# Final LayerNorm of a decoder layer in two parts: all tokens first, the last expert block's rows as a ninth tile, with the second pass of three tiles on TensorE

## What is computed

```python
def layer_norm(x, g, b):
    mu = jnp.mean(x, axis=-1, keepdims=True)
    xc = x - mu
    var = jnp.mean(xc * xc, axis=-1, keepdims=True)
    return xc * lax.rsqrt(var + LN_EPS) * g + b

m = grouped_moe(x, w_router, b_router, w_up, w_down)   # top-2 experts of each token, weighted sum
x = layer_norm(DEEPNORM_ALPHA * x + m, ln2_g, ln2_b)
```

## Time and profile before

| what | value |
|---|---|
| median of 3 runs | 1670.3 us (1667.24 to 1670.33) |
| profiled execution, its own time | 1669.88 us |
| its span (first to last instruction) | 1668.2 us |
| PE busy | 1596.2 us (96%) |
| DVE busy | 1176.0 us (70%) |
| ACT busy | 845.4 us (51%) |
| mean granted TensorE clock | 0.977 of full speed |
| last matmuls of the last block, start | 1623.15 us |
| last second pass on DVE, start | 1663.78 us |

### The profile page before, as it was taken

One profiled execution on the slowest core, in us unless ns is written; L12 is line 12 of the kernel. 1 busy time (PEld: TensorE's weight loads), 2 busy tenths in 40 slices (PEclk: granted clock), 3 DMA queues, 4 the chain that ended last, 5 costly groups with the idle time before them and its releaser, 6 DMA issues.

```text
span 1668.2 us, 20247 instructions
## 1 busy us (share of the span) xinstructions
PE 1596.2 (96%) x7711; PEld 1321.9 (79%) x7711; DVE 1176.0 (70%) x1472; ACT 845.4 (51%) x1174; POOL 183.5 (11%) x219
## 2 busy tenths in 40 slices
PE   7999999999999999999999997999999999999981
PEld 6788888888888888888788885788888888888770
DVE  3755868495666666332575666799999999998884
ACT  3113121214556555325221333688888888887773
POOL 0000000202212220000000001111111111111120
PEclk9999999999999999999999997999999999999995
DMA  5144534645232331411553566899999999999966
GB/s 160 39 82 73 128 71 85 79 73 158 80 112 66 108 87 59 145 46 49 169 176 123 174 221 235 338 369 377 370 359 357 353 353 357 351 344 365 350 237 215
DMA packets 156985, 329.29 MB, mean 197 GB/s; under 512 B 15919, under 2 KB 85551, under 8 KB 156890
## 3 DMA queue, kind: packets, MB, share of 16 engines
q1 hardware_dynamic: 140746, 289.69, 53.8%
q0 software_dynamic: 16144, 38.32, 7.7%
HBM read 296.74 MB, written 48.52 MB: 207 GB/s over the span
## 4 chain that ended last, share of the span: by engine, by line
PE 88%; DMA 6%; DVE 3%; issue 1%; SPq 1%; ACT 1%; POOLq 0%; DVEq 0%; ACTq 0%
PE ps L753 53%; PE ps L1050 26%; DMA e_raw<-in_w_down 3%; PE ps L854 2%; PE ps L839 2%; PE ps L1057 1%; DMA e_raw<-in_w_up 1%; DVE e_lo L1868 1%; PE ps L998 1%; PE ps L1063 1%; DMA x_raw<-in_x 1%; DVE zout L1928 1%; DVE zout L1921 1%; PE ps L986 0%; SPq L547 0%
## 5 line engine op out<-in xcount | busy, mean ns | idle before, releaser
L1868 DVE TENSOR_TENSOR e_lo<-e_raw,e_hi 128x1024 fp32r<-128x1024 f32 x376 | 436.2, 1221 | 24.4 <-ACT e_hi L1364 20.8
L1364 ACT ACTIVATE e_hi<-e_raw 128x1024 fp32r<-128x1024 f32 x376 | 367.8, 1050 | 25.3 <-DMA e_raw<-in_w_down 17.9
L753 PE MATMUL ps<-xt_hi,w_hi 128*128 128x512 f32 x896 | 303.3, 395 | 2.4 <-DVE xt_lo L1467 2.4
L753 PE MATMUL ps<-xt_lo,w_hi 128*128 128x512 f32 x896 | 299.0, 390 | 0.0
L753 PE MATMUL ps<-xt_hi,w_lo 128*128 128x512 f32 x896 | 298.8, 390 | 0.0
L753 PEld LDWEIGHTS ps<-xt_hi,w_lo 128*128 128x128 f32 x896 | 168.4, 188 | 35.9
L753 PEld LDWEIGHTS ps<-xt_hi,w_hi 128*128 128x128 f32 x896 | 168.3, 189 | 35.2 <-DVE xt_lo L1467 2.6
L753 PEld LDWEIGHTS ps<-xt_lo,w_hi 128*128 128x128 f32 x896 | 168.8, 188 | 33.0
L1500 DVE TENSOR_TENSOR w_lo<-w_raw,w_hi 128x512 fp32r<-128x512 f32 x136 | 94.9, 703 | 130.8 <-ACT w_hi L1133 127.4
L1133 ACT ACTIVATE w_hi<-w_raw 128x512 fp32r<-128x512 f32 x136 | 83.7, 628 | 202.1 <-PE ps L753 199.6
L1050 PE MATMUL ps<-e_hi,xe_hi 128*128 128x512 f32 x512 | 164.4, 402 | 8.5 <-DVE e_lo L1868 7.9
(11 more groups left out here) (280 smaller groups left out, 2254.7 us busy)
## 6 DMA issues: line engine op xcount, KB each, us to landing
e_raw<-in_w_up SPq DMA_DIRECT2D x128, 1024.0 KB, 21.9
e_raw<-in_w_down SPq DMA_DIRECT2D x64, 1024.0 KB, 21.7
w_raw<-in_w_in SPq DMA_DIRECT2D x64, 256.0 KB, 4.9
w_raw<-in_w_gate SPq DMA_DIRECT2D x48, 256.0 KB, 3.5
gates_d<-gate_t POOLq DMA_DIRECT2D x16, 512.0 KB, 3.4
gate_s<-gates_d SPq DMA_DIRECT2D x16, 512.0 KB, 3.6
qkv_d<-qkv POOLq DMA_DIRECT2D x12, 512.0 KB, 3.8
w_raw<-in_w_branch SPq DMA_DIRECT2D x24, 256.0 KB, 3.7
```

The costliest lines, as they stand in the source:

```text
L753: last = nc.tensor.matmul(o(h, c1 - c0), st(k), mv(k, c0, c1), start=start and k == nk[0] and n == 0, stop=h in stop and k == nk[-1] and n ...
L1364: nc.scalar.activation(e_hi[:, (UPT + s) % RSPL, :], e_raw[r][:, s % 2, :], ACT.Copy).then_inc(e_h, 1)
L1868: nc.vector.tensor_tensor(e_lo[:, sp_, :], e_raw[raw_slot(b, s)][:, s % 2, :], e_hi[:, sp_, :], ALU.subtract).then_inc(e_all, 1)
```

## The change

The final LayerNorm's start no longer waits for the last block's scatter, which is gone: the loads of the eight tiles wait for the scatters up to the block before the last one. ACT writes the last block's result to a buffer of its own, `ye_last`. POOL gathers the last block's token rows of `z_d` into `zlate`, DVE adds `ye_last`, and these rows go through the LayerNorm as a ninth tile. Its result is written by an indirect transfer over those rows of `out`, after the eight plain stores have landed. For tiles 0, 2 and 4 the second pass moves from DVE to PE: ACT makes a 128x128 matrix with the reciprocals on its diagonal (`diagonal`), PE writes b (as ones times the row b) plus that matrix times the first pass's result to PSUM, in halves of 512 columns, and ACT copies the result to `zout` (`take_z`). The stores have the order 1, 3, 0, 5, 2, 6, 7, 4. ACT's load of the square-root table moves ahead of the last `result`. Buffers move to make room (`zin`, `zout`, `zsq`, `zst`), and two semaphores are merged into others (`xg_zero`, `std9`).

```diff
+ADD_AT = 5
+ON_PE = (0, 2, 4)
+STORES = (1, 3, 0, 5, 2, 6, 7, 4)
...
-            sp.wait_ge(ye_out, 16 * (last_b + 1))
+            sp.wait_ge(e_all, item(STATIC, 0))
+            sp.wait_ge(ye_out, 16 * last_b)
             for t in range(TT):
                 sp.dma_start(zin[:, t, :], z_d[t * P:(t + 1) * P, :]).then_inc(tile_in[t], 16)
-            for t in range(TT):
-                sp.wait_ge(out_ok, t + 1)
-                sp.dma_start(out[0, t * P:(t + 1) * P, :], zout[:, t, :]).then_inc(out_dma[t % 4], 16)
+            for i, t in enumerate(STORES):
+                if t in ON_PE:
+                    sp.wait_ge(evac[0], 1 + CT * len(KINDS) // 2 + ON_PE.index(t) + 1)
+                else:
+                    sp.wait_ge(out_ok, t + 1 - sum(u < t for u in ON_PE))
+                sp.dma_start(out[0, t * P:(t + 1) * P, :], zout[t][:]).then_inc(out_dma[i % 4], 16)
...
-            for k in range(3):
+            for k in range(2):
                 scatter(tail + 1 + k)
+            pool.wait_ge(row_ok, tail + 2)
+            pool.sem_inc(passed, 1)
+            nc.gpsimd.tensor_copy(row_l[:], tok_tab[:, bass.ds(tail + 2, 1)]).then_inc(row_ok, 1)
...
+            pool.wait_ge(ye_out, 16 * (tail + 2))
+            pool.sem_inc(passed, 1)
+            nc.gpsimd.indirect_dma_start(out=zlate[:], out_offset=None, in_=z_d,
...
+            for u in range(4):
+                pool.wait_ge(out_dma[u], 16 * TT // 4)
+            pool.wait_ge(out_ok, TT + 1 - len(ON_PE))
+            nc.gpsimd.indirect_dma_start(out=out[0], out_offset=bass.IndirectOffsetOnAxis(ap=row_l[:], axis=0),
+                                         in_=zout[TT][:], in_offset=None,
...
+            for i, t in enumerate(ON_PE):
+                pe.wait_ge(z_diag, i + 1)
+                if i >= 2:
+                    pe.wait_ge(evac[0], 1 + CT * len(KINDS) // 2 + i - 1)
...
+                for h in range(2):
+                    o = ps[:, z_bank(t) + h, :]
+                    nc.tensor.matmul(o, ones_e[0:1, 0:1].to_broadcast([1, P]), lnb2[0:1, h * HALF:(h + 1) * HALF], start=True, stop=False)
+                    last = nc.tensor.matmul(o, z_rstd[i][:], zout[t][:, h * HALF:(h + 1) * HALF], start=False, stop=True)
+                last.then_inc(z_mm, 1)
...
-            result(tail + 3, UPT, 0)
-
             nc.scalar.activation(zst[:, 0, 5:6], eps[:], ACT.Sqrt)
...
+            result(tail + 3, UPT, 0, ye_last)
...
+            def diagonal(t):
+                act.wait_ge(ln9, recips(t))
+                nc.scalar.activation(z_rstd[ON_PE.index(t)][:], ident[:], ACT.Copy, scale=zst[:, t, 4:5]).then_inc(z_diag, 1)
+
+            def take_z(t):
+                act.wait_ge(z_mm, ON_PE.index(t) + 1)
+                nc.scalar.activation(zout[t][:], flat(z_bank(t)), ACT.Copy).then_inc(evac[0], 1)
+
+            deviation(0)
+            deviation(1)
+            diagonal(0)
+            deviation(2)
+            deviation(3)
+            diagonal(2)
+            deviation(4)
+            deviation(5)
+            take_z(0)
+            deviation(6)
+            diagonal(4)
+            deviation(7)
+            take_z(2)
+            deviation(TT)
+            take_z(4)
...
+            def second_pass(t):
+                dve.wait_ge(std6, TT + t + 1)
+                done.go(nc.vector.reciprocal(zst[:, t, 4:5], zst[:, t, 3:4]))
+                if t in ON_PE:
+                    assert done.n == recips(t)
+                    return
+                done.join()
+                nc.vector.scalar_tensor_tensor(zout[t][:], zout[t][:], zst[:, t, 4:5], lnb2[:], ALU.mult, ALU.add).then_inc(out_ok, 1)
...
+            for t in range(1, TT):
+                if t == ADD_AT:
+                    dve.wait_ge(late_in, 16)
...
+                    done.go(nc.vector.tensor_tensor(zlate[:], zlate[:], ye_last[:], ALU.add))
...
+                first_pass(t)
+                second_pass(t - 1)
+            second_pass(TT - 1)
+            first_pass(TT)
+            second_pass(TT)
```

More of the change, by code:

```diff
@@ L76 @@
 O_PIECE = 8
+ADD_AT = 5
+ON_PE = (0, 2, 4)
+STORES = (1, 3, 0, 5, 2, 6, 7, 4)
+LN9_ADDED = 2 * ADD_AT
 ALPHA = 2.0 ** 0.25
@@ L245, in program @@
         tok_i = at("tok_i", [P, 1], I32, 203.875)
+        row_l = at("row_l", [P, 1], I32, 205.90625)
         row_i = at("row_i", [P, 1], I32, 203.90625)
@@ L261, in program @@
         x1_scaled = at("x1_scaled", [P, D], FP32, 76)
[L262 to L265, removed]
+        zin = at("zin", [P, TT, D + 1], FP32, 79.75)
+        zlate = at("zlate", [P, D + 1], FP32, 160)
+        z_rstd = [at(f"z_rstd{i}", [P, P], FP32, 144 + i / 2) for i in range(len(ON_PE))]
+        ye_last = at("ye_last", [P, D + 1], FP32, 169)
+        zout = [at(f"zout{i}", [P, D], FP32, kb) for i, kb in enumerate((184, 188, 192, 196, 132, 136, 64, 68, 176))]
+        zsq = at("zsq", [P, D], FP32, 140)
+        zst = at("zst", [P, TT + 1, 16], FP32, 202)
         lng2 = at("lng2", [P, D], FP32, 124)
@@ L319, in program @@
         out_ok, out_dma = sem("out_ok"), [sem(f"out_dma{u}") for u in range(4)]
-        std3, std6, std9 = sem("std3"), sem("std6"), sem("std9")
+        std3, std6 = sem("std3"), sem("std6")
+        z_diag, z_mm = sem("z_diag"), sem("z_mm")
         passed = sem("passed")
@@ L351, in program, with recips, z_bank, z_tile @@
             assert raw_count(STATIC, _s) == STATIC - RTURN
+        def recips(t):
+            return 3 + 2 * t + (t + 1 >= ADD_AT)
+        def z_bank(t):
+            return 4 + 2 * (ON_PE.index(t) % 2)
+        def z_tile(t):
+            return zin[:, t, :] if t < TT else zlate[:]
         def ntiles(r):
@@ L719, in _ @@
             pool.wait_ge(y_mm, TT)
-            nc.gpsimd.memset(xg[:], 0.0).then_inc(xg_zero, 1)
+            nc.gpsimd.memset(xg[:], 0.0).then_inc(consts, 1)
             pool.sem_inc(tok_ok, NE)
@@ L723, in _ @@
             pool.wait_ge(x1_out, 16 * TT)
-            pool.wait_ge(xg_zero, 1)
+            pool.wait_ge(consts, 8)
             pool.wait_ge(r_done, 1)
@@ L1105, in _ @@
                 weights(item(last_b + 1, s), UPT + s, (ht_hi, ht_lo), s, 0, DNT)
+            for i, t in enumerate(ON_PE):
+                pe.wait_ge(z_diag, i + 1)
+                if i >= 2:
+                    pe.wait_ge(evac[0], 1 + CT * len(KINDS) // 2 + i - 1)
+                if i == 0:
+                    pe.wait_ge(par9_in, 32)
+                for h in range(2):
[3 more added lines that the diff above has]
+                last.then_inc(z_mm, 1)
         @block.scalar
@@ L1376, in split_h, with result @@
                 nc.scalar.activation(ht_hi[:], tiles(6, 1), ACT.Copy).then_inc(ht_h, 1)
-            def result(b1, extra=0, bank=2):
+            def result(b1, extra=0, bank=2, dst=ye):
                 act.wait_ge(e_used, UPT + b1 * XT + RSPL - extra)
-                if not isinstance(b1, int) or b1 > 1:
+                if dst is ye and (not isinstance(b1, int) or b1 > 1):
                     act.wait_ge(ye_out, 16 * (b1 - 1))
-                nc.scalar.activation(ye[:, 0:D], flat(bank), ACT.Copy, scale=gate_tab[:, bass.ds(b1 - 1, 1)],
-                                     accum_out=ye[:, D:D + 1]).then_inc(ye_ok, 1)
+                nc.scalar.activation(dst[:, 0:D], flat(bank), ACT.Copy, scale=gate_tab[:, bass.ds(b1 - 1, 1)],
+                                     accum_out=dst[:, D:D + 1]).then_inc(ye_ok, 1)
             def step(b):
@@ L1417, in _, with deviation @@
             result(tail + 2)
-            result(tail + 3, UPT, 0)
             nc.scalar.activation(zst[:, 0, 5:6], eps[:], ACT.Sqrt)
[L1423 to L1426, removed]
+            result(tail + 3, UPT, 0, ye_last)
+            def deviation(t):
+                z, st = z_tile(t), zst[:, t, :]
+                if t < TT:
+                    act.wait_ge(tile_in[t], 32)
+                else:
+                    act.wait_ge(ln9, LN9_ADDED)
+                nc.scalar.activation(st[:, 1:2], z[:, D:D + 1], ACT.Copy, scale=-1.0 / D).then_inc(z_mean, 1)
                 act.wait_ge(z_mean, t + 1)
-                nc.scalar.activation(zsq[:], zin[:, t, 0:D], ACT.Square, bias=st[:, 1:2], accum_out=st[:, 2:3]).then_inc(z_var, 1)
+                nc.scalar.activation(zsq[:], z[:, 0:D], ACT.Square, bias=st[:, 1:2], accum_out=st[:, 2:3]).then_inc(z_var, 1)
                 act.wait_ge(z_var, t + 1)
-                nc.scalar.activation(st[:, 3:4], st[:, 2:3], ACT.Sqrt, scale=1.0 / D, bias=eps[:]).then_inc(std9, 1)
+                nc.scalar.activation(st[:, 3:4], st[:, 2:3], ACT.Sqrt, scale=1.0 / D, bias=eps[:]).then_inc(std6, 1)
+            def diagonal(t):
[19 more added lines that the diff above has]
+            take_z(4)
         @block.vector
@@ L1917, in _, with first_pass @@
             dve.wait_ge(par9_in, 32)
[L1918 to L1928, removed]
+            done = Chain(ln9)
+            def first_pass(t):
+                dve.wait_ge(z_mean, t + 1)
```

(13 more changed lines are left out.)

9 lines of the change are left out of this document (8 added, 1 removed).

## The result

The changed kernel takes 1676.68 us (median of 5 runs, 1676.27 to 1679.34) against 1668.96 us before (five runs; the 1670.3 of the prediction was the median of the first three): 7.7 us slower, ratio 1.0048, 95% interval 1.0036 to 1.0060. The forecast was 5 us faster.

A forecast was written before the change was run, and what follows sets the result against it. Behind PE's last matmuls it saw a one-link-at-a-time relay, with DVE pacing the LayerNorm. Start -10.4, DVE's chain +1.5, stores and indirect write +3.9 gave -5.0 us: median 1665.3 from 1670.3, range 1662.0 to 1669.8.

The forecast's parts named there:

- The earlier start (-10.4): Final LayerNorm's loads wait only for the scatter before the last; first tile lands at 1633.1 instead of 1643.5.
- The late rows' gather: POOL's gather of the last block's rows lands by 1638, needed at 1644.4: hidden, with 6 us to spare.
- DVE's chain (+1.5): DVE's LayerNorm passes with new gaps at tiles 0, 1, 2, 4: 23.1 us from first tile, before 21.6.
- T: Start of ACT's first deviation in the final LayerNorm, forecast at 1633.1; later times are counted from it.
- ACT's chain: ACT's nine tiles, three diagonals, three PSUM copies and waits: last copy ends at T + 20.2, if PE is in time.
- So tile 0 takes 5.7 us for 6.2 records and 0.8 for the rest: PE's first LayerNorm tile: clock rises after 5.7 us, so it runs from T + 3.8 to T + 10.4, hidden.
- the analogy with 1623.15: PE's last block's matmuls began at 1623.15 and the clock rose 5.7 us later; the new ones were expected to match.
- case (c): Rival: PE binds because its clock stays low; no change, span end T + 35.0, median 1670.2; chance 0.10.
- The stores and the indirect write (+3.9 with the end): After DVE's end: last stores land at T + 24.7, POOL's indirect write 4.6 us later; 7.0 us instead of 3.1.
- the 3.2 us that the prediction set aside: The Trainium skill's estimate for the half-megabyte indirect write, not used; it would put the end 1.4 us earlier.
- The 0.4 between the last landing and the end of the span: Time from the indirect write's landing to the span's end, forecast as 0.4 us.
- the 0.3 for late tiles: Allowance of 0.3 us for first LayerNorm tiles landing late because the gather shares the transfer engines.

The follow-up runs named there:

- experiment 1: Changed kernel with b written as the identity times all 128 rows of the b buffer, instead of one-row matmuls: 1668.9 us, ratio to before 0.9999.
- experiment 11: Changed kernel with b by 128-row matmuls and POOL's closing drain left out at build time: 1663.34 us, ratio to before 0.9963.
- 6: Changed kernel without the matmuls that add b, so PE only multiplies with the diagonals: 1669.75 us, ratio 1.0001.
- 7: Changed kernel with b by 128-row matmuls, POOL also waiting for its late indirect write's landing before it ends: 1671.15 us.
- 10: Kernel before with only the second passes of tiles 0, 2, 4 on PE, b by 128-row matmuls, stores reordered: 1668.65 us, ratio 0.9997.
- 9: Kernel before with POOL waiting at its end for its last scatter's and all eight stores' landings, issuing nothing more: 1678.25 us, ratio 1.0049.
- 12: Changed kernel with b by 128-row matmuls and an explicit early drain on POOL before its wait for the stores: 1664.16 us, ratio 0.9970.

## Why the prediction was wrong

- **The earlier start (-10.4):** right. The load hung on the scatter before the last, and the first tile came 3.6 us after.
- **The late rows' gather:** right, hidden. It landed 7.9 us after its issue, and the addition found it there.
- **DVE's chain (+1.5):** right. Gaps at tiles 0, 1, 2 and 4 only, until PE's lateness reached the ninth tile; with that gone, T + 22.7 for T + 23.1. ACT's chain was right too: T + 19.8 for T + 20.2 in experiment 1.
- **PE: wrong in its main step.** "So tile 0 takes 5.7 us for 6.2 records and 0.8 for the rest" assumed that the clock rises once PE is busy, by the analogy with 1623.15 and with the matmuls of the earlier trace rows. All of those used 128 rows of weights. In the change half of the matmuls use one row, and the clock did not rise in 24 us. I had even noted that a one-row matmul costs the same time, and took it to be the same in every respect. It was not in time either: between one-row matmuls a record took 1.00 us at the half clock, with 128 rows everywhere 0.85 (experiment 1), and the sum had 0.92. This was case (c), given 0.10, which saw the clock stay low but not the longer records: the last copy came at T + 29.0 (T + 27.1 in the case, T + 20.2 in the sum). Worth 7.8 us by experiment 1, clock and spacing together.
- **The stores and the indirect write (+3.9 with the end):** right in total, by luck in part. From the last store's landing to the write's landing 4.4 us (4.7 forecast), but of it 1.1 to the issue, where the sum had 0.1, and 3.3 to land, where it had 4.6: two errors that cancel. The gathers were the wrong measure for the write, which moved 0.39 MB; the 3.2 us that the prediction set aside lay nearer.
- **"The 0.4 between the last landing and the end of the span": wrong.** It was 6.3 us, because the last engine to end was POOL. That POOL handed out its last transfer 34 us ahead of the span's end was in the trace of before, and so was its drain of 11.2 us; I read which instructions POOL issues, not what closes its program. No rival contained it. Worth 5.6 us: 1663.3 against 1668.9 in experiments 11 and 1.

The two terms make 13.4 us; the miss is 12.7 (7.7 slower against 5.0 faster). Without both, the sum of the prediction nearly comes out: in experiment 11, 6.2 us faster than the kernel before, for 5.0. Its profile ends at 1661.8, summed were 1663.2: T came 0.3 us earlier, the stores 0.7, the 0.3 for late tiles did not show, and the write's landing came 0.3 sooner after the stores.

The Trainium skill ("TensorE: Matmul & The Clock Gate", the section on the two states) has the clock set by how busy the engine has been recently. Experiments 1, 6, 7 and 10 agree; the changed kernel does not, if busy means a matmul in flight: PE's records stood back to back for 24 us at 0.50. The measurement decides.

The Trainium skill ("VectorE: DVE Perf Modes", "The DRAIN you can't avoid") tells of boilerplate drains of some 12 ns on all engines, from the preamble and postamble. The closing drains here are not those: they stand on a line of the kernel, and POOL's is gone when the block is built without it (experiment 11). SP's was 7 ns; POOL's was between 8.2 and 13.0 us wherever it was the first one.

What stays open: what POOL's first drain does in its 8.3 us. It is independent of transfers in flight (experiments 7 and 9) and a second drain is short (12), which fits work left over from the transfers of the whole kernel and a cost that the first drain has in any case; the two were not told apart. Nor was it tried how many rows are enough for the clock, whether the rows of the weights, those of the data or the repeated single element count, how large a part of the matmuls may be such, or why the weight loads of the change stand at the matmuls' starts.

## What to carry to other kernels

When a change gives an engine the last word, read how that engine's program ends, not only its last instruction: POOL ending late costs some 6 us behind the landing of a transfer just issued, 8 us with none in flight, unless a drain is placed early, where POOL waits anyway, or left out where semaphores cover its transfers. One-row matmuls between full ones kept TensorE at its half clock here and cost 0.3 us a matmul besides, so a cheap-looking row broadcast was better written with a full matrix. And a change of several parts is best summed part by part, as each part's price can then be checked alone: here the part that was to help most was sound, and two side effects hid it.

## What was unexpected of the hardware

- Matmuls of 512 float32 columns, back to back: 2.00 us each over 24 us at a granted clock of 0.50, when every second one has one row of weights; when all have 128, 1.71 us at 0.50 and 0.86 us at 1.00, from the fourth one on in experiment 1.
- POOL's closing drain: 9.5 us with an indirect write just issued (1667.4 to 1677.0), 8.9 with a direct one, 8.3 after waiting for the landing, 8.2 after 34 us without a transfer, 3.6 when another drain went before.
